# Masking the attention scores with one more matmul instead of inside the scan

## The chip, the cores and the metric

One Trainium2 chip, one core of it. The metric is the device time of one execution in microseconds (us), input and output in device memory. The kernel before takes 1345.78 us, the median of three runs.

## The reference, cut to what matters

One decoder layer on 1024 tokens of width 1024: RMS norm, a projection to six blocks of 512 columns, a short convolution on three of them and an attention with 8 heads of 64 on the other three, an output projection, then a mixture of experts. The change touches the attention alone:

```
for blk in range(S // Q_BLOCK):                       # 8 blocks of 128 queries
    z = einsum('bhqd,bhkd->bhqk', qb, kb) * scale     # keys 0 .. L-1, L = t0 + 128
    mask = s_idx < t_idx                              # strictly before the query
    log_keep = where(mask, log_sigmoid(-z), 0.0)
    shifted = concatenate([log_keep[..., 1:], 0])
    suffix = cumsum(shifted, axis=3, reverse=True)
    A = where(mask, exp(log_sigmoid(z) + suffix), 0.0)
    out = einsum('bhqk,bhkd->bhqd', A, vb)
```

So the weight of key s for query t is sigmoid(z_s) times the product of sigmoid(-z_j) over s < j < t, and zero for s >= t. The mask cuts only the last 128 keys of a block of queries, the ones at its diagonal.

## The kernel before

The program is a row of blocks with a barrier between them: projections with the attention, output projection with the router, dispatch, experts, combination. The first block holds all that the change touches.

The attention is cut into 64 units. Unit n belongs to a pair of heads p = n // 16, a block of queries t = n % 16 // 2 and a head h = n % 2 of the pair. Its length is (t + 1) * 128 keys: eight units of each length from 128 to 1024. For each unit

- TensorE computes the scores (`scores`, L442 to L444): three matmuls for each stretch of at most 512 keys (high by high, high by low, low by high part of the float32 values), with the 64 rows of one head as contraction. The last stretch is 128, 256, 384 or 512 keys wide, and its last matmul announces the scores.
- ScalarE (`open_unit`, L586 and L587, or L593 and L594 where the two stretches don't lie side by side in PSUM) writes sigmoid(z) to `soft` and sigmoid(-z) to `kept`. For 54 of the 64 units that is one pair of instructions.
- VectorE (`weigh`) runs a scan from the last key to the first over `kept` (L735), which leaves in each column the product of all to its right, and multiplies `soft` by it (L737). The tile `start_at` has 1 at the diagonal of its last 128 columns and 0 elsewhere. The scan's state is max(kept * state, start_at) and starts at 0, so it stays 0 right of the diagonal and starts from 1 there: this is the mask. All units lie at the right end of `soft`, whose last column is set to 0 once.
- TensorE transposes the weights 128 columns at a time (`turn`, L454), ScalarE copies them out of PSUM (L602), and TensorE multiplies them with v (`values`, L464).

TensorE's order is written out by hand. In turn n it issues the scores of unit n + 1, the values of unit n - 2, the transposes of unit n - 1 and then some matmuls of the input projection (`project`, L406, 128x512), of which a table deals out 10, 11, 16 or 20 to a turn and none to the last four. At one place in each pair of heads (`JOIN`) the norms of the next pair's q and k and of finished rows are made: TensorE sums them (L416, L422, L429), ScalarE changes its table of functions (L501) and takes logarithms and exponentials, and the scores of the next units wait there.

At the start of the program GpSimd makes the constants (L335 to L347); TensorE and ScalarE wait for seven steps of it.

Of the kernel before, what the change touches and what calls it, by code (L numbers as in the profile page):

```python
# [14 lines left out]
F32 = mybir.dt.float32  # L15
F32R = mybir.dt.float32r
# [27 lines left out]
def hymba_moe_layer(nc, x, norm_mix_w, w_in, conv_w, q_norm_w, k_norm_w, group_norm_conv_w,  # L44
                    group_norm_attn_w, w_out, norm_ffn_w, w_group, b_group, w_expert, b_expert,
                    w1, w3, w2, out):
    S, D = x.shape[1], x.shape[2]
# [30 lines left out]
    with ExitStack() as ctx:  # L78
        sem = lambda name: ctx.enter_context(nc.semaphore(name))
# [2 lines left out]
        psf = ps.rearrange("p a b -> p (a b)")  # L82

        base = (nc.sbuf_base + 31) // 32 * 32
        ROOM = 207 * KIB
        ctx.enter_context(nc.sbuf_tensor("arena", [P, ROOM // 4], F32))
        names = set()

# [27 lines left out]
        q_lo = [at(f"q_lo{i}", 84 + 16 * i, [P, S], F32R) for i in range(2)]  # L116
        k_hi = [at(f"k_hi{i}", 88 + 16 * i, [P, S], F32R) for i in range(2)]
# [3 lines left out]
        soft = [at(f"soft{i}", 112 + 4 * i, [P, S]) for i in range(2)]  # L121
        kept = [at(f"kept{i}", 120 + 4 * i, [P, S]) for i in range(2)]
# [59 lines left out]
        consts_in = sem("consts_in")  # L182
        g1_in = sem("g1_in")
        consts_made = sem("consts_made")
        soft_ends = sem("soft_ends")
# [40 lines left out]
        z_read = sem("z_read")  # L226
        multiplied = sem("multiplied")
        weighed = sem("weighed")
# [58 lines left out]
        with nc.Block(no_gpsimd_drain=True) as block:  # L287
# [44 lines left out]

            @block.gpsimd
            def _(pool):
                pool.memset(start_at, 0.0).then_inc(consts_made, 1)  # L335
                pool.memset(same_head, 0.0).then_inc(consts_made, 1)
                for b in range(2):
                    pool.memset(soft[b][:, S - 1:S], 0.0).then_inc(soft_ends, 1)
                pool.memset(eps, EPS).then_inc(consts_made, 1)
                pool.memset(u[:, 0:TAPS - 1], 0.0).then_inc(consts_made, 1)  # L340
                pool.wait_ge(consts_made, 4)
                pool.affine_select(out=ident, in_=ident, compare_op=ALU.not_equal, fill=1.0, base=0,
                                   pattern=[[-1, P]], channel_multiplier=1).then_inc(consts_made, 1)
                pool.wait_ge(consts_made, 5)
                pool.memset(same_head[0:HD, 0:HD], 1.0).then_inc(consts_made, 1)
                pool.wait_ge(consts_made, 6)
                pool.memset(same_head[HD:P, HD:P], 1.0).then_inc(consts_made, 1)  # L347
                pool.wait_ge(consts_made, 7)

                def chunk_hi(c):  # L350
                    pool.wait_ge(w_landed[c % 2], 16 * (c // 2 + 1))
                    pool.tensor_copy(w_hi[c % 2], w_raw[c % 2]).then_inc(w_hi_made, 1)

                def keys_hi(r):
                    pool.wait_ge(k_scaled, r + 1)
                    pool.tensor_copy(k_hi[r % 2], k_new[r % 2]).then_inc(k_hi_made, 1)

                for c in range(PRE):
                    chunk_hi(c)
                for p in range(NPAIR):  # L360
                    keys_hi(p)
                    for c in range(PRE + 4 * p, PRE + 4 * p + 4):
                        chunk_hi(c)
                for c in range(2 * CB):
                    if c % 2 == 0:
                        pool.wait_ge(w_out_in[c // 2], 16)
                    pool.tensor_copy(w_out_hi[:, c], w_out_raw[:, c]).then_inc(w_out_hi_made, 1)

            @block.tensor
            def _(pe):  # L370
# [60 lines left out]
                def scores(n):  # L431
                    p, t, h = n // PU, n % PU // 2, n % 2
                    rows = slice(h * HD, (h + 1) * HD)
                    cols = slice(t * P, (t + 1) * P)
                    if n % PU == 0:
                        pe.wait_ge(k_ready, p + 1)
                    for c0 in range(0, length(n), BANK):
                        c1 = min(c0 + BANK, length(n))
                        use = z_first[n] + c0 // BANK
                        pe.wait_ge(z_read, use - 2)  # L440
                        z = Z(use)[:, 0:c1 - c0]
                        pe.matmul(z, q_hi[p % 2][rows, cols], k_hi[p % 2][rows, c0:c1], start=True, stop=False)  # L442
                        pe.matmul(z, q_hi[p % 2][rows, cols], k_lo[p % 2][rows, c0:c1], start=False, stop=False)
                        mm = pe.matmul(z, q_lo[p % 2][rows, cols], k_hi[p % 2][rows, c0:c1], start=False, stop=True)  # L444
                    mm.then_inc(scored, 1)

                def turn(n):
                    pe.wait_ge(weighed, n + 1)
                    for hf in range(halves(n)):
                        g = th[n] + hf  # L450
                        if g >= 2:
                            pe.wait_ge(turned_read, g - 1)
                        for j in range(4 * hf, min(4 * hf + 4, length(n) // P)):
                            mm = pe.transpose(TB(g)[:, (j % 4) * P:(j % 4 + 1) * P], soft[n % 2][:, S - length(n) + j * P:S - length(n) + (j + 1) * P], ident)  # L454
                        mm.then_inc(turned, 1)

                def values(n):
# [10 lines left out]
                pe.wait_ge(consts_made, 7)  # L468
                turn_x(0)
                for m in range(NT):  # L470
                    if m + 1 < NT:
# [27 lines left out]
            def _(act):  # L499
# [74 lines left out]
                def open_unit(n):  # L574
                    p, t, h = n // PU, n % PU // 2, n % 2
                    act.wait_ge(scored, n + 1)
                    if n % PU == 0:
                        act.wait_ge(q_minus_made, p + 1)
                    if n >= 2:
                        act.wait_ge(turned, th[n - 1])  # L580
                    up, down = q_scale[p % 2][:, t, h:h + 1], q_minus[p % 2][:, t, h:h + 1]
                    s, k = soft[n % 2][:, S - length(n):], kept[n % 2][:, S - length(n):]
                    b = z_first[n] % 3
                    if b + halves(n) <= 3:
                        z = psf[:, b * BANK:b * BANK + length(n)]
                        act.activation(s[:, 0:length(n) - 1], z[:, 0:length(n) - 1], ACT.Sigmoid, scale=up)  # L586
                        act.activation(k, z, ACT.Sigmoid, scale=down).then_inc(z_read, halves(n))  # L587
                    else:
                        for hf in range(2):
                            c0, c1 = hf * BANK, min((hf + 1) * BANK, length(n))  # L590
                            z = Z(z_first[n] + hf)
                            last = min(c1, length(n) - 1)
                            act.activation(s[:, c0:last], z[:, 0:last - c0], ACT.Sigmoid, scale=up)  # L593
                            act.activation(k[:, c0:c1], z[:, 0:c1 - c0], ACT.Sigmoid, scale=down).then_inc(z_read, 1)  # L594

                def take_turned(n):
                    for hf in range(halves(n)):
# [11 lines left out]
                act.wait_ge(consts_made, 7)  # L609
                square_x(0)  # L610
                square_x(1)
                for i in range(4):
# [46 lines left out]
            def _(dve):  # L659
# [65 lines left out]
                        dve.scalar_tensor_tensor(y_mix[:, row], y_mix[:, row], row_gain(row), sq, ALU.mult, ALU.mult).then_inc(rows_scaled, 1)  # L725

                def weigh(n):

                    L = length(n)
                    s, k, one = soft[n % 2][:, S - L:], kept[n % 2][:, S - L:], start_at[:, S - L:]  # L730
                    if n == 0:
                        dve.wait_ge(soft_ends, 2)
# [845 lines left out]
```

## Time and profile before

| | before |
|---|---|
| median of 3 runs | 1345.78 us (1343.4 to 1346.09) |
| the profiled execution's own time | 1346.09 us |
| its span, first to last instruction | 1344.4 us |
| TensorE busy | 1196.3 us, 89% |
| VectorE busy | 870.1 us, 65% |
| ScalarE busy | 732.0 us, 54% |
| GpSimd busy | 146.7 us, 11% |

The time of an execution is some 1.7 us more than its span. A matmul is busy from its start to its modelled end, and neighbours overlap: what a matmul costs TensorE in a stream is the distance from its start to the start of the next, not its duration. The attention's units run from 116 to 546 us of the span; the experts take most of the time from 620 us on.

### The profile page before, as it was taken

The page shows a single profiled execution, that of the slowest core. Times are in us where ns is not written, and L with a number is a line of the kernel's source. Part 1 is how long each engine was busy: PE and PEld are TensorE (multiplying, and loading weights), DVE is VectorE, ACT ScalarE, POOL GpSimd, SP SyncE. Part 2 cuts the span into 40 slices and gives each one's busy share as a digit, 9 for nine tenths or more (in the row PEclk, how much of TensorE's full clock was granted, in tenths as well). Part 3 has the DMA queues.
Part 4 walks back from the last instruction along what each step waited for, and adds up shares of the span by engine and source line. Part 5 has one row for each costly group of instructions (what it writes and reads, how often), then busy time and mean ns, then how long its engine had stood idle before and what let it go on. Part 6 is the DMA issues. An engine that isn't in the chain of part 4 may idle for free. (4 is left out here: it accounts for less than half of the span.)

```text
span 1344.4 us, 16647 instructions
## 1 busy us (share of the span) xinstructions
PE 1196.3 (89%) x5806; PEld 968.3 (72%) x5806; DVE 870.1 (65%) x910; ACT 732.0 (54%) x918; POOL 146.7 (11%) x193
## 2 busy tenths in 40 slices
PE   5999979969989997899837999999999999999930
PEld 4887767747767775688716888888888888888820
DVE  4414444435435453723166999999999999999926
ACT  4322534543454236211206888888888888888810
POOL 1000000000000003100010111111111111111000
PEclk9999989979999999899857999999999999999975
DMA  6111100100000003611155999999999999999409
GB/s 203 37 32 32 32 16 16 32 16 17 16 16 23 28 14 125 265 49 48 39 249 196 357 389 384 381 382 380 384 384 385 382 386 378 384 384 388 174 17 374
DMA packets 57338, 261.88 MB, mean 195 GB/s; under 512 B 13008, under 2 KB 33488, under 8 KB 43984
## 3 DMA queue, kind: packets, MB, share of 16 engines
q1 hardware_dynamic: 46928, 240.31, 46.9%
q0 software_dynamic: 9216, 16.80, 3.3%
q10 hardware_dynamic: 1152, 4.19, 0.8%
q8 instruction: 28, 0.46, 0.1%
q14 instruction: 14, 0.11, 0.0%
HBM read 252.88 MB, written 25.17 MB: 207 GB/s over the span
## 5 line engine op out<-in xcount | busy, mean ns | idle before, releaser
L1250 DVE TENSOR_TENSOR e_lo<-W,e_hi 128x1024 fp32r<-128x1024 f32 x384 | 452.6, 1221 | 25.6 <-ACT e_hi L1244 22.5
L1244 ACT ACTIVATE e_hi<-W 128x1024 fp32r<-128x1024 f32 x384 | 403.3, 1060 | 96.8 <-PE ps L1215 94.0
L735 DVE TENSOR_TENSOR_SCAN kept<-kept,start_at 128x128 f32<-128x128 f32 (+7 forms) x64 | 88.7, 1385 | 210.7 <-ACT kept L587 177.6
L1213 PE MATMUL ps<-e_hi,xT_hi 128*128 128x512 f32 x512 | 204.2, 399 | 7.1 <-DVE e_lo L1250 7.1
L1215 PE MATMUL ps<-e_lo,xT_hi 128*128 128x512 f32 x512 | 201.5, 394 | 0.0
L1214 PE MATMUL ps<-e_hi,xT_lo 128*128 128x512 f32 x512 | 201.0, 393 | 0.0
L406 PE MATMUL ps<-xnT_hi,w_hi 128*128 128x512 f32 x320 | 128.4, 401 | 15.2 <-DVE u L699 7.1
L586 ACT ACTIVATE soft<-ps,q_scale 128x127 f32<-128x127 f32 (+7 forms) x54 | 38.0, 704 | 186.4 <-PE ps L454 175.6
L406 PE MATMUL ps<-xnT_hi,w_lo 128*128 128x512 f32 x320 | 127.9, 400 | 0.0
L406 PE MATMUL ps<-xnT_lo,w_hi 128*128 128x512 f32 x320 | 127.7, 399 | 0.0
L1213 PEld LDWEIGHTS ps<-e_hi,xT_hi 128*128 128x128 f32 x512 | 97.6, 191 | 27.0 <-issue 4.0
L1215 PEld LDWEIGHTS ps<-e_lo,xT_hi 128*128 128x128 f32 x512 | 97.1, 190 | 20.9
L1214 PEld LDWEIGHTS ps<-e_hi,xT_lo 128*128 128x128 f32 x512 | 97.2, 190 | 19.4
L1213 PE MATMUL ps<-e_hi,hidT_hi 128*128 128x512 f32 x256 | 103.0, 403 | 2.7 <-DVE e_lo L1250 2.7
L1215 PE MATMUL ps<-e_lo,hidT_hi 128*128 128x512 f32 x256 | 100.4, 392 | 0.0
L1214 PE MATMUL ps<-e_hi,hidT_lo 128*128 128x512 f32 x256 | 100.4, 392 | 0.0
L464 PE MATMUL ps<-probsT,v 128*64 128x128 f32 x576 | 84.5, 297 | 9.7 <-ACT probsT L602 9.7
L464 PEld LDWEIGHTS ps<-probsT,v 128*64 128x64 f32 x576 | 68.2, 148 | 26.3 <-issue 12.5
L1307 POOL DMA_INDIRECT y_rows<-y,idx_pair x32 | 32.6, 1020 | 458.4 <-ACT y L1270 458.4
L406 PEld LDWEIGHTS ps<-xnT_hi,w_hi 128*128 128x128 f32 x320 | 60.8, 190 | 28.1 <-issue 16.6
L406 PEld LDWEIGHTS ps<-xnT_lo,w_hi 128*128 128x128 f32 x320 | 61.0, 191 | 11.8 <-issue 0.2
L406 PEld LDWEIGHTS ps<-xnT_hi,w_lo 128*128 128x128 f32 x320 | 61.0, 191 | 11.7
(207 smaller groups left out, 1768.2 us busy)
## 6 DMA issues: line engine op xcount, KB each, us to landing
W<-in_w_dram SPq DMA_DIRECT2D x96, 2048.0 KB, 10.7
w_raw<-in_w_in_dram SPq DMA_DIRECT2D x20, 512.0 KB, 4.0
yy<-y_rows SPq DMA_DIRECT2D x8, 1024.0 KB, 13.6
xt<-in_x_dram SPq DMA_DIRECT2D x8, 512.0 KB, 3.8
w_out_raw<-in_w_out_dram SPq DMA_DIRECT2D x4, 1024.0 KB, 9.4
xn_rows<-xn SPq DMA_DIRECT2D x8, 512.0 KB, 2.6
out_dram<-x ACTq DMA_DIRECT2D x8, 512.0 KB, 9.0
x<-in_x_dram SPq DMA_DIRECT2D x1, 3072.0 KB, 14.9
```

Of the source, the lines that this page charges most:

```text
L406: mm = pe.matmul(ps[:, 6 + g % 2], w, r, start=(i % TICKS == 0), stop=(i % TICKS == TICKS - 1))
L464: mm = pe.matmul(ps[h * HD:(h + 1) * HD, VB, (t % 4) * P:(t % 4 + 1) * P], v[:, j, head], probsT[:, j, :], start=(j == 0), stop=(j == t))
L586: act.activation(s[:, 0:length(n) - 1], z[:, 0:length(n) - 1], ACT.Sigmoid, scale=up)
L735: dve.tensor_tensor_scan(back, back, one[:, ::-1], 0.0, ALU.mult, ALU.max).then_inc(multiplied, 1)
L1213: pe.matmul(o, xs_hi[:, k], e_hi[:, p, cols], start=(k == 0), stop=False)
L1214: pe.matmul(o, xs_lo[:, k], e_hi[:, p, cols], start=False, stop=False)
L1215: mm = pe.matmul(o, xs_hi[:, k], e_lo[:, p, cols], start=False, stop=(k == last))
L1244: act.activation(e_hi[:, p], flat[:, p * D:(p + 1) * D], ACT.Copy).then_inc(s["hi_made"], 1)
L1250: dve.tensor_tensor(e_lo[:, p], flat[:, p * D:(p + 1) * D], e_hi[:, p], ALU.subtract).then_inc(s["lo_made"], 1)
L1307: pool.indirect_dma_start(out=y_rows, out_offset=bass.IndirectOffsetOnAxis(ap=idx_pair[b].bitcast(U32), axis=0), in_=y[b], in_offset=None, ...
```

## The change

The mask moves from VectorE's scan to TensorE. Two more constants are made, `identr` (the identity) and `maskr` (-1e30 on and above the diagonal, 0 below), both 128x128 in the type fp32r that the scores' matmuls use. Behind the scores of each unit one more matmul adds `maskr` to the last 128 columns: the masked scores are so low that sigmoid(z) is 0 and sigmoid(-z) is 1 there. The scan then starts at 1, has `kept` as both operands and takes the minimum (of a product and one of its factors, which is the product). `start_at` and the semaphore `soft_ends` go; units lie at the left end of `soft` and `kept`; the arena is 2 KiB smaller. The waits for the constants go from 7 to 10.

```
-        start_at = keep("start_at", [P, S])
-        ident = start_at[:, S - P:S]
+        ident = keep("ident", [P, P])
         same_head = keep("same_head", [P, P])
+        identr = keep("identr", [P, P], F32R)
+        maskr = keep("maskr", [P, P], F32R)
...
-                pool.memset(start_at, 0.0).then_inc(consts_made, 1)
+                pool.memset(ident, 0.0).then_inc(consts_made, 1)
+                pool.memset(maskr.bitcast(F32), 0.0).then_inc(consts_made, 1)
...
+                pool.wait_ge(consts_made, 8)
+                pool.tensor_copy(identr, ident).then_inc(consts_made, 1)
+                pool.affine_select(out=maskr, in_=maskr.bitcast(F32), compare_op=ALU.is_gt, fill=MASKED, base=0,
+                                   pattern=[[-1, P]], channel_multiplier=1).then_inc(consts_made, 1)
...
-                        mm = pe.matmul(z, q_lo[p % 2][rows, cols], k_hi[p % 2][rows, c0:c1], start=False, stop=True)
+                        pe.matmul(z, q_lo[p % 2][rows, cols], k_hi[p % 2][rows, c0:c1], start=False, stop=(c1 < length(n)))
+                    mm = pe.matmul(z[:, c1 - c0 - P:c1 - c0], identr, maskr, start=False, stop=True)
                     mm.then_inc(scored, 1)
...
-                        act.activation(s[:, 0:length(n) - 1], z[:, 0:length(n) - 1], ACT.Sigmoid, scale=up)
-                        act.activation(k, z, ACT.Sigmoid, scale=down).then_inc(z_read, halves(n))
+                        act.activation(soft[n % 2][:, 0:length(n)], z, ACT.Sigmoid, scale=up)
+                        act.activation(kept[n % 2][:, 0:length(n)], z, ACT.Sigmoid, scale=down).then_inc(z_read, halves(n))
...
-                    back = k[:, ::-1]
-                    dve.tensor_tensor_scan(back, back, one[:, ::-1], 0.0, ALU.mult, ALU.max).then_inc(multiplied, 1)
+                    back = k[:, L - 1::-1]
+                    dve.tensor_tensor_scan(back, back, back, 1.0, ALU.mult, ALU.min).then_inc(multiplied, 1)
                     dve.wait_ge(multiplied, n + 1)
-                    dve.tensor_tensor(s[:, :L - 1], s[:, :L - 1], k[:, 1:], ALU.mult).then_inc(weighed, 1)
+                    dve.tensor_tensor(s[:, :L - 1], s[:, :L - 1], k[:, 1:L], ALU.mult).then_inc(weighed, 1)
```

## Rows read from the trace of the kernel before

**Rows 1.** The page's 40 slices of the span: TensorE busy and its granted clock.
```profile
PE   5999979969989997899837999999999999999930
PEclk9999989979999999899857999999999999999975
```

**Rows 2.** Busy time by stretch, four stretches of the attention; columns in the first row.
```profile
core 0: us, PE busy (x) PEld busy (x) DVE busy (x) ACT busy (x) POOL busy (x), PEclk, DMA share, GB/s
...
201.00:262.00 61.00, 60.66 (x333) 46.62 (x331) 27.64 (x29) 27.93 (x55) 2.08 (x2) 1.00 0.09 25
262.00:312.00 50.00, 38.86 (x165) 28.84 (x166) 17.82 (x15) 21.96 (x34) 3.40 (x3) 0.80 0.04 12
...
410.00:511.00 101.00, 100.67 (x542) 78.70 (x541) 51.27 (x50) 36.00 (x67) 5.50 (x4) 1.00 0.07 22
511.00:547.00 36.00, 25.97 (x132) 19.05 (x130) 15.78 (x11) 22.50 (x32) 13.36 (x9) 0.86 0.25 102
```

**Rows 3.** Who waited for whom: TensorE, 110 to 546 us; total, times, longest.
```profile
PE ps L464 <- ACT probsT L602: 9.7, 7, 3.9
PE ps L442 <- ACT kept L587: 8.2, 2, 4.1
```

**Rows 4.** The timeline of TensorE's matmuls, one unit of 640 keys: start, duration.
```profile
146.30 0.39 PE L444 MATMUL ps<-k_hi,q_lo 64*128 64x512 f32 x1
146.53 0.22 PE L442 MATMUL ps<-k_hi,q_hi 64*128 64x128 f32 x1
146.59 0.27 PE L443 MATMUL ps<-k_lo,q_hi 64*128 64x128 f32 x1
146.70 0.27 PE L444 MATMUL ps<-k_hi,q_lo 64*128 64x128 f32 x1
146.90 0.87 PE L464 MATMUL ps<-probsT,v 128*64 128x128 f32 x6
```

**Rows 5.** The timeline of the weight loads in the same unit.
```profile
146.30 0.18 PEld L442 LDWEIGHTS ps<-k_hi,q_hi 64*128 64x128 f32 x1
146.53 0.18 PEld L443 LDWEIGHTS ps<-k_lo,q_hi 64*128 64x128 f32 x1
146.64 0.19 PEld L444 LDWEIGHTS ps<-k_hi,q_lo 64*128 64x128 f32 x1
```

**Rows 6.** The timeline of TensorE's matmuls where a unit's last stretch is 512 wide.
```profile
240.69 0.39 PE L444 MATMUL ps<-k_hi,q_lo 64*128 64x512 f32 x1
241.01 0.65 PE L464 MATMUL ps<-probsT,v 128*64 128x128 f32 x4
```

**Rows 7.** The timeline at the second pair's join; the wait before stands in brackets.
```profile
284.74 0.90 ACT L586 ACTIVATE soft<-ps,q_scale 128x767 f32<-128x767 f32 x1
...
286.48 0.68 PE L442 MATMUL ps<-k_hi,q_hi 64*128 64x384 f32 x1 [4.08 <-ACT kept L587]
286.96 0.52 PE L443 MATMUL ps<-k_lo,q_hi 64*128 64x384 f32 x1
287.28 0.52 PE L444 MATMUL ps<-k_hi,q_lo 64*128 64x384 f32 x1
```

**Rows 8.** Groups of instructions by line and shape, 90 to 560 us: VectorE's `weigh`.
```profile
L735 DVE TENSOR_TENSOR_SCAN kept<-kept,start_at 128x1024 f32<-128x1024 f32 x8 | 18.4, 2299 | 26.2 <-ACT kept L587 21.1 <-ACT kept L594 5.1
...
L737 DVE TENSOR_TENSOR soft<-soft,kept 128x1023 f32<-128x1023 f32 x8 | 10.4, 1306 | 0.3
...
L735 DVE TENSOR_TENSOR_SCAN kept<-kept,start_at 128x128 f32<-128x128 f32 x8 | 5.0, 625 | 16.2 <-ACT kept L587 16.2
```

**Rows 9.** The timeline of the program's start.
```profile
0.84 0.95 POOL L335 MEMSET start_at<- 128x1024 f32 x1 [0.29 <-POOLq L1573]
...
2.31 0.28 POOL L342 TENSOR_SCALAR_AFFINE_SELECT start_at<-start_at 128x128 f32<-128x128 f32 x1 [0.24 <-POOL u L340]
...
2.86 0.15 POOL L347 MEMSET same_head<- 64x64 f32 x1
...
4.08 1.28 ACT L506 ACT_TABLE_LOAD   x1 [4.08 <-DMA xt<-in_x_dram]
```

More of the change, by code:

```diff
@@ L184, in hymba_moe_layer @@
         consts_made = sem("consts_made")
-        soft_ends = sem("soft_ends")
         x_landed = [sem(f"x_landed{i}") for i in range(2)]
@@ L334, in _ @@
             def _(pool):
-                pool.memset(start_at, 0.0).then_inc(consts_made, 1)
+                pool.memset(ident, 0.0).then_inc(consts_made, 1)
+                pool.memset(maskr.bitcast(F32), 0.0).then_inc(consts_made, 1)
                 pool.memset(same_head, 0.0).then_inc(consts_made, 1)
-                for b in range(2):
-                    pool.memset(soft[b][:, S - 1:S], 0.0).then_inc(soft_ends, 1)
                 pool.memset(eps, EPS).then_inc(consts_made, 1)
                 pool.memset(u[:, 0:TAPS - 1], 0.0).then_inc(consts_made, 1)
-                pool.wait_ge(consts_made, 4)
+                pool.wait_ge(consts_made, 5)
                 pool.affine_select(out=ident, in_=ident, compare_op=ALU.not_equal, fill=1.0, base=0,
                                    pattern=[[-1, P]], channel_multiplier=1).then_inc(consts_made, 1)
-                pool.wait_ge(consts_made, 5)
+                pool.wait_ge(consts_made, 6)
                 pool.memset(same_head[0:HD, 0:HD], 1.0).then_inc(consts_made, 1)
-                pool.wait_ge(consts_made, 6)
+                pool.wait_ge(consts_made, 7)
                 pool.memset(same_head[HD:P, HD:P], 1.0).then_inc(consts_made, 1)
-                pool.wait_ge(consts_made, 7)
+                pool.wait_ge(consts_made, 8)
+                pool.tensor_copy(identr, ident).then_inc(consts_made, 1)
+                pool.affine_select(out=maskr, in_=maskr.bitcast(F32), compare_op=ALU.is_gt, fill=MASKED, base=0,
+                                   pattern=[[-1, P]], channel_multiplier=1).then_inc(consts_made, 1)
                 def chunk_hi(c):
@@ L453, in turn @@
                         for j in range(4 * hf, min(4 * hf + 4, length(n) // P)):
-                            mm = pe.transpose(TB(g)[:, (j % 4) * P:(j % 4 + 1) * P], soft[n % 2][:, S - length(n) + j * P:S - length(n) + (j + 1) * P], ident)
+                            mm = pe.transpose(TB(g)[:, (j % 4) * P:(j % 4 + 1) * P], soft[n % 2][:, j * P:(j + 1) * P], ident)
                         mm.then_inc(turned, 1)
@@ L466, in values @@
                     mm.then_inc(valued, 1)
-                pe.wait_ge(consts_made, 7)
+                pe.wait_ge(consts_made, 10)
                 turn_x(0)
@@ L581, in open_unit @@
                     up, down = q_scale[p % 2][:, t, h:h + 1], q_minus[p % 2][:, t, h:h + 1]
-                    s, k = soft[n % 2][:, S - length(n):], kept[n % 2][:, S - length(n):]
                     b = z_first[n] % 3
@@ L585, in open_unit @@
                         z = psf[:, b * BANK:b * BANK + length(n)]
-                        act.activation(s[:, 0:length(n) - 1], z[:, 0:length(n) - 1], ACT.Sigmoid, scale=up)
-                        act.activation(k, z, ACT.Sigmoid, scale=down).then_inc(z_read, halves(n))
+                        act.activation(soft[n % 2][:, 0:length(n)], z, ACT.Sigmoid, scale=up)
+                        act.activation(kept[n % 2][:, 0:length(n)], z, ACT.Sigmoid, scale=down).then_inc(z_read, halves(n))
                     else:
                         for hf in range(2):
[L590 to L594, printed above, removed]
+                            cols = slice(hf * BANK, min((hf + 1) * BANK, length(n)))
+                            z = Z(z_first[n] + hf)[:, 0:cols.stop - cols.start]
+                            act.activation(soft[n % 2][:, cols], z, ACT.Sigmoid, scale=up)
+                            act.activation(kept[n % 2][:, cols], z, ACT.Sigmoid, scale=down).then_inc(z_read, 1)
                 def take_turned(n):
@@ L727, in weigh @@
                 def weigh(n):
[L729 to L732, printed above, removed]
+                    s, k, L = soft[n % 2], kept[n % 2], length(n)
                     dve.wait_ge(z_read, z_first[n] + halves(n))
-                    back = k[:, ::-1]
-                    dve.tensor_tensor_scan(back, back, one[:, ::-1], 0.0, ALU.mult, ALU.max).then_inc(multiplied, 1)
+                    back = k[:, L - 1::-1]
+                    dve.tensor_tensor_scan(back, back, back, 1.0, ALU.mult, ALU.min).then_inc(multiplied, 1)
                     dve.wait_ge(multiplied, n + 1)
-                    dve.tensor_tensor(s[:, :L - 1], s[:, :L - 1], k[:, 1:], ALU.mult).then_inc(weighed, 1)
+                    dve.tensor_tensor(s[:, :L - 1], s[:, :L - 1], k[:, 1:L], ALU.mult).then_inc(weighed, 1)
                 dve.wait_ge(g1_in, 16)
```

4 lines of the change are left out of this document (2 added, 2 removed).

## The prediction, made before the changed kernel was run

> **What bounds the kernel now.** I read the page's slices first, for where TensorE is full and at which clock. It is busy nine tenths and more of most slices, with dips in the attention's part [rows 1]. The stretches tell the two kinds of attention apart: from 201 to 262 us TensorE is busy 60.66 of 61.00 us, from 410 to 511 us 100.67 of 101.00, both at granted clock 1.00 (2.4 GHz), while VectorE and ScalarE are busy at most half of the time. From 262 to 312 us and from 511 to 547 us, a join and the end, it is busy 38.86 of 50.00 and 25.97 of 36.00 us, at 0.80 and 0.86, a mix of 2.4 and 1.2 GHz [rows 2]. So in the plain run of units TensorE sets the pace and a nanosecond added to its stream is a nanosecond of time, and VectorE's scan is off the path. At the joins and at the end the pace is that of a chain through ScalarE and VectorE. The view of waits says the same: TensorE's long waits are few, two of 4.1 us each for `kept` and seven for `probsT` with 9.7 us in all [rows 3].
>
> What a small matmul costs must come from starts. The timeline of one unit of 640 keys shows all the cases. The 512-wide L444 is followed by the next start after 0.23 us (146.30 to 146.53). The first 128-wide one, whose weights were loaded while L444 ran (load at 146.30), is followed after 0.06 us (146.53 to 146.59). The next is followed after 0.11 us (146.59 to 146.70), as its own weights could only be loaded behind that one (load at 146.53, the next at 146.64). The last is followed after 0.20 us by the values, which stand behind a wait [rows 4, 5]. That wait costs 0.09 us over the stream: a 512-wide L444 in front of it is followed after 0.32 us (240.69 to 241.01) instead of 0.23 [rows 4, 6].
>
> **The change, part by part.**
>
> *The extra matmul, 64 times.* It has 128 columns and the full 128x128 weights. Nothing stands between L444 and it, so its weights can load while L444 runs, as those of the 128-wide L442 did. Behind it stands the wait that stood behind L444.
>
> - Last stretch 256, 384 or 512 wide (48 units): L444 is long enough to hide the load of 0.11 us, so the extra matmul adds its own streaming, 0.06 us. 48 x 0.06 = 2.9 us.
> - Last stretch 128 wide (16 units, lengths 128 and 640): L444 is too short to hide it, and the pace is 0.11 us. 16 x 0.11 = 1.8 us.
>
> Together 4.7 us. Off this go units whose extra matmul falls into a wait. At the join L444 of one unit ends long before ScalarE opens it at 284.74 us, and TensorE then waits 4.08 us [rows 7]: one such unit at each of the three joins with a next pair (the fourth has none behind it), and two at the end, where the turns have no projection to do and TensorE idles 10 us [rows 2]. 5 x 0.06 = 0.3 us off. To it come the units that run at half clock behind such a wait, where 384 columns take 0.32 us (286.96 to 287.28) [rows 7]; that is 0.11 us for 128 columns instead of 0.06. Some six of them, 6 x 0.05 = 0.3 us. The two cancel, and the sum stays at 4.7 us.
>
> The bounds: if every one of the 64 costs the load's pace, 64 x 0.11 = 7.0 us. If only the streaming counts and all of some 15 units around the joins and at the end are covered, 49 x 0.06 = 2.9 us. Neither holds a penalty for going from 64 rows of contraction to 128 and back. The trace has such a step only across a wait (L444 to L464), at the same 0.09 us that L444 of any width pays there, so I take none. The upper end keeps it: the load exposed behind L444 adds another 64 x 0.11, for 0.06 + 0.11 = 0.17 us a unit, 10.9 us.
>
> Of this load the Trainium skill ("TensorE: Matmul & The Clock Gate", section "The mechanism") says that it overlaps a running matmul only when the two use different row groups. The trace speaks against it: L442's 64-row load starts at 146.30, together with the 64-row L444, and its matmul follows at L444's full pace [rows 4, 5]. By the skill's rule the load would be exposed each time, which is the 10.9 us of the rival below; by the row it is hidden.
>
> *The longer chain.* The scores are announced 0.06 to 0.11 us later. ScalarE doesn't wait for them in the plain run: it opens a unit when the transposes two units back are done, which TensorE issues behind these scores and the values. Those cover it, and ScalarE is busy 27.93 of 61.00 us there [rows 2]. Where the cover is gone, at the joins, the extra matmul is in the sum already.
>
> *ScalarE.* One column more in 64 of its instructions (128x1024 for 128x1023): nothing that a row can show, and behind TensorE.
>
> *The scan.* Same length, same number of streams read, same start and end. It takes 2299 ns for 1024 columns and L737 1306 ns for 1023 with as many operands [rows 8]. Going from 128 to 1024 columns costs 1674 ns, 1.87 ns a column. I take no change. Bounds: if reading `kept` twice brought it to L737's time, 1.0 us less for the longest; if a clash of the two reads cost as much, 1.0 us more. In the plain run either is hidden behind TensorE; it counts only at the joins and the end, for two or three scans each, 10 scans in all and so at most 10 us either way.
>
> *The constants.* GpSimd's first memset of 0.95 us shrinks to an eighth of its columns, and one memset, one copy and one select of 128 columns come, the select at 0.28 us by its like. GpSimd's last step ended at 3.01 us, and ScalarE's first work waits for x until 4.08 us [rows 9]. Three steps of at most 0.3 us, even without the saving, end by 3.91 us: nothing. Without that cover it would be 0.1 us, 0.9 less the 0.8 saved. VectorE's wait for `soft_ends` had long been met.
>
> *After the attention.* The next block begins behind a barrier, and the experts' weights are asked for there, so the delay is passed on whole.
>
> **The sum.** 1346.09 us of the profiled execution plus 4.7 is 1350.8. That execution is the slowest of three, 0.3 us over their median of 1345.78, so I forecast 1350.5 us. About 0.2%, 2.7 us, is what a measurement of this kernel can tell from no change.
>
> **The rivals.**
>
> - *The load is not hidden.* L444 uses 64 rows, `identr` all 128; if the weights can't go in while a matmul on part of the rows runs, each unit costs 0.17 us: 10.9 us, 1356.7. For it: no row shows a step from 64 to 128 rows without a wait. Against it: the loads of rows 5 run under matmuls on the same rows. It decides from 0.11 us a unit on.
> - *It lands in slack.* TensorE idles 11.1 us in the join shown and 10.0 us at the end [rows 2], with two more joins at most some 43 us, and a delay in front of a wait can be absorbed. If a third of the extra matmuls fell there, and the last units' turns were paced by ScalarE, 43 x 0.06 = 2.6 us would be left: within 0.2%, 1348.4. For it: the waits of rows 3. Against it: they sit at four places, and rows 2 give TensorE 99.4% and more between them.
> - *The scan gets shorter* (the other side). If its pace is set by reading two tiles, reading one tile twice could bring it to 1306 ns. The joins and the end are chains through it: 10 scans x 1.0 us = 10 us off, plus 4.7, is 1340.5. It decides once a long scan loses over 0.7 us. Against it: L737 also reads two tiles, one column a step, in 1306 ns, so the reading of two tiles is not what makes 2299.
>
>   The Trainium skill ("DVE: opcode table, instruction layouts, handler registers and perf-mode slots", section "Datapath and trigger behaviour") says that the scan routes its state back a stage and runs at half throughput; the trace agrees in direction, with 1.87 ns a column against at most 1.28 (1306 / 1023) for L737. By that rule nothing about the operands helps, and the scan stays at 2299.
>
> **Chances.** The sum as worked out 0.55; the load exposed, or a like penalty for the step in rows, 0.17; slack 0.22; a shorter scan or another gain 0.06. The forecast is the first. The first case has its own range from 1348.7 (2.9 us) to 1352.8 (7.0 us). For 8 in 10 the range must reach into slack below and most of the way to the exposed load above: 1347.0 to 1357.0. Slower by over 0.2%: the first two cases, 0.72. Within 0.2%: 0.22. Faster: 0.06.
>
> **What the profile after would show.** 64 more matmuls of 128x128 with a start 0.23 us behind a 512-wide L444, and the values 0.15 us behind them (0.20 behind a 128-wide L444). If the load is exposed, its start lies 0.34 us behind. The scans at 2299 and 625 ns, by length. The first values matmul of the stretch from 410 to 511 us comes later by as many small steps as units lie before it, and the block's end by 4 to 5 us; after that every stage keeps its length. The prediction is wrong if the scan changes by over 0.1 us, if the waits of rows 3 shrink by what the matmuls add, or if the clock at a join falls or rises at another place: 10 us of full-clock work that runs at half clock instead costs 10 us more.

## The result, and the profile after

The changed kernel takes 1354.05 us, the median of 5 runs (1353.19 to 1359.11), where the kernel before takes 1345.36 us beside it. The ratio is 1.0081, with a 95% interval of 1.0057 to 1.0104. That is 8.7 us slower. I had forecast 1350.5 us in a range from 1347.0 to 1357.0, so the direction and the range held, and the cost is almost twice the 4.7 us of the sum.

The page of the changed kernel, its slices as in [rows 1]:

```profile
span 1359.5 us, 16775 instructions
PE   6999989979998998799945999999999999999930
PEclk9999969988998998899956999999999999999975
```

The profiled execution took 1361.15 us, the longest of those seen, 15.1 us over that of before. So the span can't be compared with the median above; why executions of this kernel differ so much is taken up with the experiments. The stretches of [rows 2], in the changed kernel:

```profile
core 0: us, PE busy (x) PEld busy (x) DVE busy (x) ACT busy (x) POOL busy (x), PEclk, DMA share, GB/s
...
160.00:201.00 41.00, 35.31 (x147) 27.21 (x146) 13.47 (x12) 15.12 (x25) 3.27 (x3) 0.76 0.05 14
201.00:262.00 61.00, 60.88 (x324) 46.54 (x322) 26.44 (x27) 27.04 (x55) 2.86 (x2) 0.99 0.06 18
...
410.00:511.00 101.00, 96.32 (x497) 74.70 (x498) 50.05 (x48) 36.48 (x67) 6.29 (x4) 0.97 0.07 21
```

TensorE is as full as before from 201 to 262 us, with fewer matmuls in the stretch (324 for 333). The units are the same, so each takes longer. The stretch from 410 to 511 us now holds part of a join, which has moved later, and can't be compared with its row of before. The last step of the attention, ScalarE's copy of the last output, shows the sum of it, in the timeline of before and then of the changed kernel:

```profile
545.96 0.60 ACT L607 ACTIVATE y_mix<-ps 128x512 f32<-128x512 f32 x1 [2.05 <-PE ps L464]
```

```profile
563.22 0.60 ACT L607 ACTIVATE y_mix<-ps 128x512 f32<-128x512 f32 x1 [2.05 <-PE ps L466]
```

The attention ends 17.3 us later. The spans differ by 15.1 us, so 2.2 us come back in the stages behind. There the trace has TensorE at half clock for 114.6 us before and for 109.9 us here. By the two levels these 4.7 us are worth at most 2.3 us, near the difference; more on this stands with the second profile below.

The timeline of TensorE's matmuls in the unit of 640 keys, as in [rows 4], tells what the extra matmul (L446) costs:

```profile
146.69 0.39 PE L445 MATMUL ps<-k_hi,q_lo 64*128 64x512 f32 x1
146.92 0.22 PE L443 MATMUL ps<-k_hi,q_hi 64*128 64x128 f32 x1
146.98 0.27 PE L444 MATMUL ps<-k_lo,q_hi 64*128 64x128 f32 x1
147.09 0.27 PE L445 MATMUL ps<-k_hi,q_lo 64*128 64x128 f32 x1
147.29 0.33 PE L446 MATMUL ps<-maskr,identr 128*128 128x128 f32 x1
147.55 0.87 PE L466 MATMUL ps<-probsT,v 128*64 128x128 f32 x6
```

And the weight loads there, as in [rows 5]:

```profile
147.03 0.19 PEld L445 LDWEIGHTS ps<-k_hi,q_lo 64*128 64x128 f32 x1
147.29 0.19 PEld L446 LDWEIGHTS ps<-maskr,identr 128*128 128x128 f32 x1
```

L446 starts 0.20 us behind L445, as the values did before it, and the values start 0.26 us behind L446. No wait stands in front of L446, and still its load begins only at 147.29, with the matmul itself, and not under L445. In a unit whose last stretch is 384 wide the two steps are 0.26 and 0.26 us:

```profile
243.15 0.33 PE L445 MATMUL ps<-k_hi,q_lo 64*128 64x384 f32 x1
243.41 0.33 PE L446 MATMUL ps<-maskr,identr 128*128 128x128 f32 x1
243.67 0.65 PE L466 MATMUL ps<-probsT,v 128*64 128x128 f32 x4
```

So a unit pays 0.26 us whatever its width, and 64 of them 16.6 us. TensorE's waits, as in [rows 3], have shrunk (the view goes from 110 to 560 us):

```profile
PE ps L466 <- ACT probsT L602: 7.7, 4, 3.6
...
PE ps L443 <- ACT kept L588: 6.9, 2, 3.4
```

The attention ends at 564 us here, and up to there `probsT` has 8.3 us in 5 waits. So the two shrank by 1.4 and 1.3 us, and all rows of this view together from 36.7 us to 31.4.

The scan of 1024 columns kept its length, 2364 ns on the mean where [rows 8] have 2299. That of 128 columns has a mean of 736 ns for 625, over the 0.1 us that I had named as a sign of being wrong. But most single ones take 0.42 us in both kernels, and the mean is moved by a few long ones (two of 1.2 us before; four of 0.8 to 1.3 us here), whose number differs from profile to profile. The second experiment shows that the scan costs no time.

### The profile page after: what moved, and what is told of

The parts are those of the page before. It is cut to its first block and busy times, and to the rows that moved or that the text cites. A ratio compares the mean times of both kernels' runs of the same rounds, so it can differ in the third digit from the quotient of the medians.

```text
span 1359.5 us, 16775 instructions
## 1 busy us (share of the span) xinstructions
PE 1218.1 (90%) x5870; PEld 984.5 (72%) x5870; DVE 871.8 (64%) x910; ACT 732.6 (54%) x918; POOL 146.9 (11%) x194
## 5 line engine op out<-in xcount | busy, mean ns | idle before, releaser
L731 DVE TENSOR_TENSOR_SCAN kept<-kept 128x128 f32<-128x128 f32 (+7 forms) x64 | 91.0, 1422 | 228.6 <-ACT kept L588 191.7
L587 ACT ACTIVATE soft<-ps,q_scale 128x128 f32<-128x128 f32 (+7 forms) x54 | 38.1, 705 | 200.4 <-PE ps L456 189.2
L407 PE MATMUL ps<-xnT_hi,w_hi 128*128 128x512 f32 x320 | 128.9, 403 | 14.4 <-DVE u L699 6.9
L353 POOL CAST w_hi<-w_raw 128x1024 fp32r<-128x1024 f32 x20 | 24.8, 1238 | 421.7 <-DMA w_raw<-in_w_in_dram 421.7
```

The costliest lines, as they stand in the source:

```text
L407: mm = pe.matmul(ps[:, 6 + g % 2], w, r, start=(i % TICKS == 0), stop=(i % TICKS == TICKS - 1))
L587: act.activation(soft[n % 2][:, 0:length(n)], z, ACT.Sigmoid, scale=up)
L731: dve.tensor_tensor_scan(back, back, back, 1.0, ALU.mult, ALU.min).then_inc(multiplied, 1)
```

## The experiments

**Which part costs.** The first kernel adds only the extra matmul and its constants to the kernel before. The second takes only the extra matmul out of the changed kernel.

```
# e1, on the kernel before
-                        mm = pe.matmul(z, q_lo[p % 2][rows, cols], k_hi[p % 2][rows, c0:c1], start=False, stop=True)
+                        pe.matmul(z, q_lo[p % 2][rows, cols], k_hi[p % 2][rows, c0:c1], start=False, stop=(c1 < length(n)))
+                    mm = pe.matmul(z[:, c1 - c0 - P:c1 - c0], identr, maskr, start=False, stop=True)

# e2, on the changed kernel
-                        pe.matmul(z, q_lo[p % 2][rows, cols], k_hi[p % 2][rows, c0:c1], start=False, stop=(c1 < length(n)))
-                    mm = pe.matmul(z[:, c1 - c0 - P:c1 - c0], identr, maskr, start=False, stop=True)
+                        mm = pe.matmul(z, q_lo[p % 2][rows, cols], k_hi[p % 2][rows, c0:c1], start=False, stop=True)
```

> The kernel before with the extra matmul and its two constants alone; scan, alignment and start_at as before. Theory A (the extra matmul is all of the loss; it starts 0.20 us behind a 128-wide last matmul and 0.32 us behind a 512-wide one, as if a wait stood between, and is followed after 0.26 us): the same gaps, attention's end 16 to 18 us later than before in the profiled execution, and the time that of the changed kernel within 2 us, 1352 to 1360 us. Theory B (a part of the loss lies in the scan's new operands or the left alignment): the same gaps, but at least 3 us less time than the changed kernel.

> The changed kernel without the extra matmul: the mask is left out of the computation, so keys at and behind the diagonal count. Theory A: 1344 to 1347 us, as before, and scans as in the changed kernel (2.3 us for 1024 columns). Theory B: 3 us or more over before.

With the matmul alone: 1356.97 us, ratio 1.0098 (1.0081 to 1.0115). Without it: 1343.67 us beside 1343.83 of before, ratio 0.9999 (0.9989 to 1.0009). The gaps of the first are those expected (0.20, 0.32 and 0.26 us). Two numbers of theory A were missed: its median lies 2.9 us over that of the changed kernel, where I had allowed 2, and its attention ends 15.3 us later than before, not 16 to 18. B wanted a shorter time than the changed kernel's, so A holds. The scan's new operands and the left alignment cost nothing that can be measured, nor do the constants; the extra matmul is the whole loss.

**Why 0.26 us.** In the third kernel the extra matmul contracts over the head's 64 rows, as the scores do:

```
-                    mm = pe.matmul(z[:, c1 - c0 - P:c1 - c0], identr, maskr, start=False, stop=True)
+                    mm = pe.matmul(z[:, c1 - c0 - P:c1 - c0], identr[rows], maskr[rows], start=False, stop=True)
```

> The extra matmul contracts over the 64 rows of the head instead of 128: half of the queries' masks are left out, and the instruction count stays. Theory C (the step from 64 to 128 rows is what keeps the weights from loading early): the extra matmul starts 0.23 us behind a 512-wide one and is followed after 0.15 us, 0.06 to 0.11 us a unit, some 5 us in all, 1349 to 1352 us. Theory D (any short matmul behind the scores costs this, by its width or its constant operands): 0.26 us a unit as in the changed kernel, 1353 us or more.

1348.01 us, ratio 1.0035 (1.0021 to 1.0049), 4.2 us more than before. Its timeline, same unit:

```profile
145.64 0.27 PE L444 MATMUL ps<-k_lo,q_hi 64*128 64x128 f32 x1
145.75 0.27 PE L445 MATMUL ps<-k_hi,q_lo 64*128 64x128 f32 x1
145.87 0.27 PE L446 MATMUL ps<-maskr,identr 64*128 64x128 f32 x1
146.07 0.87 PE L466 MATMUL ps<-probsT,v 128*64 128x128 f32 x6
```

0.12 us to L446 and 0.20 from it: where one step of 0.20 us stood there are now two, and the unit pays 0.11 to 0.12 us. In units with a wider last stretch it pays 0.06 us (behind a 512-wide L445 the steps are 0.23 and 0.15 us, where one of 0.32 stood). These are the prices of my sum, and the total of 4.2 us is near its 4.7, if 1 us under the range of theory C. With one shape for the scores and the extra matmul the sum is right; what was wrong is that a change of shape is free. Theory C holds over D, which would have the same loss here.

The fourth kernel moves the full matmul between the values (128x64) and the transposes (128x128):

```
+                def mask(n):
+                    wide = length(n) - (halves(n) - 1) * BANK
+                    z = Z(z_first[n] + halves(n) - 1)
+                    pe.matmul(z[:, wide - P:wide], identr, maskr, start=False, stop=True).then_inc(scored, 1)
...
                     if n >= 2:
                         values(n - 2)
+                    if r != JOIN[p] + 1 and n + 1 < UNITS:
+                        mask(n + 1)
                     if n:
                         turn(n - 1)
```

> The extra matmul of each unit moved behind the values (128 rows, 64 columns) and ahead of the transposes (128 rows); it computes the same. Theory C: no step in rows is added, its weights load under the values, and it costs 0.06 to 0.11 us a unit: 1349 to 1352 us. Theory D: 0.26 us a unit, 1353 us or more. By either, ScalarE opens its units no later, as it waits for the transposes behind.

1352.18 us, ratio 1.0061 (1.0041 to 1.0080), between the two theories' ranges. The timeline (L450 is the extra matmul):

```profile
244.04 0.65 PE L469 MATMUL ps<-probsT,v 128*64 128x128 f32 x4
244.62 0.33 PE L450 MATMUL ps<-maskr,identr 128*128 128x128 f32 x1
244.79 0.41 PE L459 MATMUL ps<-ident,soft 128*128 128x128 f32 x2
```

L450 starts 0.58 us behind the values and stands 0.17 us ahead of the transposes. But the transposes behind it are shortened: before, they stood first behind the values, and the second of them followed the first after 0.16 us; here it follows after 0.13. Over the whole turn, from its first scores matmul to its third projection matmul, it is 2.46 us where before has 2.32:

```profile
240.12 0.49 PE L442 MATMUL ps<-k_hi,q_hi 64*128 64x512 f32 x1
...
241.59 0.55 PE L454 MATMUL ps<-start_at,soft 128*128 128x128 f32 x3
...
242.44 0.39 PE L406 MATMUL ps<-xnT_hi,w_hi 128*128 128x512 f32 x1
```

The unit pays 0.13 us, and 64 of them 8.5 us, near the measured loss of 8.4 us.

Theory C as I had put it, the step in rows alone, is too narrow. The values and L450 both have 128 rows, but the values load 64 columns of weights and L450 loads 128, and L450's load isn't hidden: it starts only with the matmul, at 244.62. The kernel before has this change too, in front of its transposes. So L450 adds no change, it only moves to where one is.

The 0.09 us that I had put down to waits doesn't belong to them either. Between L450 and the transposes stands a wait for VectorE, and the step is 0.17 us, the load's 0.11 and the streaming's 0.06, without the 0.09. In the changed kernel no wait stands between L445 and L446, and there the 0.09 us is paid (0.32 us behind a 512-wide one for 0.23). What stands at both places where it was paid, here and in [rows 4, 6], is a change of shape. The kernel before had shown a wait without the price, even in the rows that I had read: its code has a wait for ScalarE (`z_read`) in front of each stretch of scores, so also in front of the L442 at 146.53 us, and that starts after the plain 0.23 us [rows 4]. It is the same at 163.52 us, behind another wait for ScalarE and with one shape on both sides:

```profile
163.29 0.40 PE L406 MATMUL ps<-xnT_lo,w_hi 128*128 128x512 f32 x1
163.52 0.84 PE L416 MATMUL ps<-same_head,q_sq 128*128 128x2 f32 x7
```

So, theory E: each change of shape costs 0.09 us and a weight load in the open, whether there is a wait or not. The Trainium skill says the first half of it: "Changing tiling mode (not just tile) drains the TensorE" ("TensorEngine Tiling (Array Packing)", section "Key Properties", under "Tiling Modes"). The trace agrees, and its price here is 0.09 us for the drain, up to 0.11 us more for the load of 128 columns and 0.05 us for one of 64. This page spoke against the change, and I hadn't weighed it.

The next two kernels put the extra matmul where both neighbours are 128x128: behind the transposes, and behind the first projection matmul of the turn.

```
# e5
                     if n:
                         turn(n - 1)
+                    if r != JOIN[p] + 1 and n + 1 < UNITS:
+                        mask(n + 1)
                     project(ticks_by(n - 1), ticks_by(n))

# e6
+                    first = min(ticks_by(n - 1) + 1, ticks_by(n))
+                    project(ticks_by(n - 1), first)
+                    if r != JOIN[p] + 1 and n + 1 < UNITS:
+                        mask(n + 1)
+                    project(first, ticks_by(n))
```

> The extra matmul moved behind the transposes and ahead of the projection; both are 128x128, and it computes the same. Theory E (each change of the tile's shape on TensorE costs a start delayed by 0.09 us and a weight load of 0.11 us that isn't hidden, wait or no wait; the extra matmul between 64x128 and 128x64 adds one such change): here it adds none and costs only the pace of a weight load, 0.11 us a unit; 64 x 0.11 = 7.0 us at most, 1348 to 1352 us. Theory W (the 0.09 us is the price of a wait and only a step in rows hides no load): as before the move behind the values, 0.16 us a unit, 1352 us or more.

> The extra matmul moved behind the first projection matmul of the turn, 512 wide, under which its weights load. Theory E: 0.06 us a unit, some 3.5 us in all, 1346 to 1349 us, less than behind the transposes. Theory W: 0.11 us or more a unit, 1350 us or more.

Behind the transposes: 1348.75 us, ratio 1.0031 (1.0017 to 1.0044), in E's range and under W's. The same unit as above, from its scores to the third projection matmul, takes 2.43 us for 2.32:

```profile
239.53 0.49 PE L443 MATMUL ps<-k_hi,q_hi 64*128 64x512 f32 x1
...
241.00 0.55 PE L459 MATMUL ps<-ident,soft 128*128 128x128 f32 x3
241.31 0.31 PE L450 MATMUL ps<-maskr,identr 128*128 128x128 f32 x1
241.45 0.44 PE L407 MATMUL ps<-xnT_lo,w_hi 128*128 128x512 f32 x1
241.73 0.39 PE L407 MATMUL ps<-xnT_hi,w_lo 128*128 128x512 f32 x1
241.96 0.40 PE L407 MATMUL ps<-xnT_hi,w_hi 128*128 128x512 f32 x1
```

That is E's 0.11 us a unit. In the projection: 1354.01 us, ratio 1.0070 (1.0052 to 1.0088). This is over E's range; by the letter it is W's expectation that came in, though W is out by the step from L445 to L446. Its timeline:

```profile
241.60 0.48 PE L407 MATMUL ps<-xnT_lo,w_hi 128*128 128x512 f32 x1
241.91 0.22 PE L450 MATMUL ps<-maskr,identr 128*128 128x128 f32 x1
241.97 0.44 PE L407 MATMUL ps<-xnT_hi,w_lo 128*128 128x512 f32 x1
242.25 0.39 PE L407 MATMUL ps<-xnT_hi,w_hi 128*128 128x512 f32 x1
```

The extra matmul is followed after 0.06 us, as expected. But the next one, 512 wide, is followed after 0.28 us and not 0.23: its weights had only 0.06 us of cover. In a stream of one shape the price of a short matmul is the pace of a load, 0.11 us; a wide one in front only moves it to the one behind. (In e3 it was 0.06 us, but there a change of shape stood behind it, whose load is in the open anyway.) That makes it equal to e5, and not 5 us worse. Most of the 5 us goes with the clock, which comes below.

The eighth kernel issues the extra matmul twice in a row:

> Two extra matmuls in a row behind the scores (the mask is added twice, which computes the same). Theory E: the second adds no change of shape, only the pace of a weight load, 0.11 us a unit, 5 to 7 us over the changed kernel. Theory D (each such matmul costs 0.26 us by itself): 14 to 17 us over it.

1360.05 us, ratio 1.0111 (1.0093 to 1.0130): 5.5 us over the same kernel with one, timed beside it, at a higher mean granted clock (0.945 against 0.943). Its timeline:

```profile
246.52 0.39 PE L445 MATMUL ps<-k_hi,q_lo 64*128 64x512 f32 x1
246.84 0.33 PE L446 MATMUL ps<-maskr,identr 128*128 128x128 f32 x1
247.01 0.28 PE L447 MATMUL ps<-maskr,identr 128*128 128x128 f32 x1
247.22 0.65 PE L467 MATMUL ps<-probsT,v 128*64 128x128 f32 x4
```

From the first extra matmul to the values it is now 0.38 us (0.17 and 0.21) where it was 0.26, 0.12 more: the first carries its own load and its streaming, the second the pace of a load, and the drain is paid once. D, 0.26 us for each, is out.

One table puts the prices together by the turn, so without the clock's share. It compares the turns that run outside the joins, 52 of them, each with the same turn of the kernel before, from the first scores matmul to the third projection matmul; the second column is the turn shown above, of a unit with 512 keys.

| | that turn | over before, median of 52 | times 64 | median time over before |
|---|---|---|---|---|
| before | 2.32 us | | | |
| changed kernel | 2.58 us | 0.26 us | 16.6 us | 8.7 and 9.7 us |
| e3, 64 rows | 2.38 us | 0.06 us | 4.6 us, with 0.11 for 16 of them | 4.2 us |
| e4, behind the values | 2.46 us | 0.13 us | 8.5 us | 8.4 us |
| e5, behind the transposes | 2.43 us | 0.11 us | 7.2 us | 3.9 us |
| e6, in the projection | 2.43 us | 0.11 us | 7.0 us | 9.2 us |
| e8, twice | 2.68 us | 0.36 us | 23.3 us | 15.2 us |

Without the extra matmul (e2) the median over before is 0. The last two columns differ by what waits take up and by the clock.

**Why executions differ.** The changed kernel was run again.

> The changed kernel once more, for another profile. Theory G (its executions differ, 1353 to 1361 us, by how long TensorE's clock is granted at half): an execution near 1354 us has a mean granted clock of 0.944 to 0.945 and in its profile some 10 us less at half clock, in the attention or right behind it; one near 1360 us has 0.938. Theory H (they differ by something else, as transfers): times and clock don't go together.

1354.58 us, ratio 1.0071 (1.0053 to 1.0089). Here are all ten executions of the changed kernel, profiled ones included, with the mean granted clock of each:

```
us      1353.19 1353.79 1353.81 1354.05 1354.53 1354.64 1356.99 1358.26 1359.11 1361.15
clock   0.944   0.944   0.945   0.944   0.944   0.943   0.942   0.941   0.940   0.938
```

They go together, with a correlation of -0.98, and 0.001 of clock is worth 1.2 us. That is near what the two levels give: 0.001 of 1355 us is 2.7 us more at 1.2 GHz, and each such microsecond of full work costs half a microsecond more, 1.4 us. The kernel before stays between 0.939 and 0.942 in all 13 executions timed beside these, 1344.8 us on the mean. Its own times there, 1342.1 to 1347.5 us, don't go with the clock; in the two other groups of its executions, with clocks from 0.937 to 0.945, they do in part (correlations -0.60 and -0.73). At its 0.940 to 0.941 the changed kernel takes 1358.3 to 1359.1 us, 13.5 to 14.4 us more than before. The median shows 8.7 because more than half of the executions were granted the full clock for longer.

The second profile, of the execution of 1356.99 us, shows where. The same stretch as above, the first join:

```profile
160.00:201.00 41.00, 34.62 (x158) 26.32 (x157) 15.13 (x13) 17.23 (x28) 4.06 (x3) 0.88 0.05 14
```

Clock 0.88 for 0.76 is 10 us less at half clock ((0.88 - 0.76) x 2 x 41), and 11 more matmuls fit into the stretch. In the first profile TensorE runs at half clock twice here, for 6.8 us from 178 us on and for 13.7 us from 188 us on; in the second once, for 10.2 us from 187 us on. In both it had idled 0.46 us just before 178 us, and only in one did the clock fall there. Theory G holds. What decides it in an execution isn't settled: the program is the same. It also explains most of e6: its four executions had 0.939 to 0.940, those of e5 0.943 on the mean, which is 4 us.

The second profile also compares best with that of before, whose clock in this stretch is 0.88 too:

```profile
160.00:201.00 41.00, 33.98 (x163) 25.99 (x162) 16.63 (x15) 16.43 (x28) 3.74 (x3) 0.88 0.05 14
```

In both traces TensorE is at half clock for 47.8 us of the attention. The attention ends 13.5 us later (559.48 us for 545.96), the 16.6 us of the extra matmuls less what the waits take up. The stages behind it come in two lengths in the 13 profiles of this record, 798.0 to 798.4 us with 114.2 to 114.6 us at half clock and 795.7 to 796.2 us with 109.9 to 110.6 us. The profile of before has the long one, that of the changed kernel the short one both times. It isn't the extra matmul that decides it: e6, which has it, and e2, which hasn't, both have the long one.

**A version with fewer changes of shape.** A turn of the kernel before goes 128x128 (projection), 64x128 (scores), 128x64 (values), 128x128 (transposes): three changes, 64 times. The last three kernels leave mask and scan as before and do the two heads of one block of queries in the same turn where the buffers allow it: the values of units up to 512 keys (their transposed weights share one tile, half each), the scores of units of 256 to 512 keys, and both.

```
# e9: values of two heads
+        in_pair = lambda n: n % PU < 8
+        probs_at = lambda n: 4 * (n % 2) if in_pair(n) else 0
...
-                        values(n - 2)
+                        if not in_pair(n - 2):
+                            values(n - 2)
+                        elif n % 2:
+                            values(n - 3)
+                            values(n - 2)
...
-                            act.wait_ge(valued, n)
+                            act.wait_ge(valued, n - 1 if 1 <= n % PU < 8 else n)

# e10: scores of two heads
...
+                    pe.wait_ge(z_read, z_first[n + 1] - 2)
+                    for term, (q, k) in enumerate(((q_hi, k_hi), (q_hi, k_lo), (q_lo, k_hi))):
+                        for h in range(2):
+                            rows = slice(h * HD, (h + 1) * HD)
+                            mm = pe.matmul(Z(z_first[n + h])[:, 0:length(n)], q[p % 2][rows, cols], k[p % 2][rows, 0:length(n)],
+                                           start=(term == 0), stop=(term == 2))
...
```

> The kernel before, mask in the scan, with the values of two heads done in one turn for units of up to 512 keys; the same instructions, 16 changes of tile shape fewer (128x64 between 64x128 and 128x128). Theory E (a change of shape costs a start delayed by 0.09 us and a load that isn't hidden, 0.05 us for 64 columns): 0.14 us a pair, 2.2 us less attention in the profile, in equal steps of 0.14 us; the time 1342 to 1344 us where before gives 1345. Theory W (the price belongs to the waits): as many waits are left out, so this gives the same; against it speaks that transposes to projection has a wait and no price. If nothing is gained, the price is hidden by something else.

> The kernel before with the scores of both heads in one turn for the 24 units of 256 to 512 keys that share a block of queries, their matmuls taking turns between the upper and the lower 64 rows. Theory E: 12 changes of shape fewer at 0.20 us, 2.4 us less. Theory R (matmuls on different halves of the rows run side by side, as the two starts 0.05 us apart at the join of the kernel before): another 0.35 to 0.69 us a pair, 6 us, so 8 us less in all, about 1337 us. Without R, 1342 to 1343 us.

> Both together. By E and R the two gains add, 10 to 11 us less attention in the profile and a time near 1335 us; by E without R 4 to 5 us less. If ScalarE or VectorE becomes the bound for the short units, less than the sum of the two.

| | median | ratio to before | interval |
|---|---|---|---|
| values in pairs | 1338.97 us | 0.9949 | 0.9932 to 0.9967 |
| scores in pairs | 1334.25 us | 0.9922 | 0.9898 to 0.9946 |
| both | 1326.25 us | 0.9865 | 0.9839 to 0.9890 |

All three are faster than both kernels, the last by 18.8 us than before. The gains add up, or a little more. Each is larger than expected. For the scores I had expected both heads to run side by side, and they do: six matmuls take the 0.89 us that three took (237.39 to 238.28), two starting together.

```profile
237.39 0.50 PE L454 MATMUL ps<-k_hi,q_hi 64*128 64x512 f32 x2
237.72 0.40 PE L454 MATMUL ps<-k_lo,q_hi 64*128 64x512 f32 x2
237.96 0.39 PE L454 MATMUL ps<-k_hi,q_lo 64*128 64x512 f32 x2
238.28 0.65 PE L476 MATMUL ps<-probsT,v 128*64 128x128 f32 x4
```

For the values I had counted only the changes of shape, 2.2 us. The timeline of the kernel with values in pairs shows the rest:

```profile
235.22 0.67 PE L466 MATMUL ps<-probsT,v 128*64 128x128 f32 x8
235.82 0.55 PE L456 MATMUL ps<-start_at,soft 128*128 128x128 f32 x3
```

Eight matmuls of two heads take 0.60 us, where four of one head took 0.58 in the kernel before (from 241.01 us [rows 6] to the transposes at 241.59) and in e4: heads that write different halves of the output partitions run side by side too, even though the program issues all of one head first. The Trainium skill says that different tiles load and multiply in parallel (same page, same section); the trace agrees, 8 in 0.60 us. For longer units less of it overlaps: the 12 matmuls of two heads with 384 keys take 1.08 us where six took 0.80, and the 16 of two heads with 512 keys 1.51 us where eight took 1.02. A pair saves 0.36, 0.57, 0.52 and 0.52 us from 128 to 512 keys, 7.9 us for all 16. The median gained 6.1 us, at a mean clock 0.001 under that of before. With both in pairs there is one more gain: 12 turns then have neither scores nor values, so no change of shape at all, and their transposes start 0.23 us behind the last projection matmul. So these three kernels don't price a change of shape alone; the changed kernel, e3 and e8 do.

## Why the prediction was right, and where it was off

- *TensorE sets the pace in the plain run of units.* Right. The whole loss came from its stream, and e2 shows that nothing else of the change costs time.
- *The price of the extra matmul.* This is the step that failed: "Nothing stands between L444 and it, so its weights can load while L444 runs", and with it "That wait costs 0.09 us over the stream". There is a change of shape between them. It costs 0.09 us, and the load is in the open. The term that I put at 0.06 to 0.11 us measured 0.26 us (0.09 + 0.11 + 0.06), and 64 x 0.26 is 16.6 us where the sum had 4.7. I read the 0.09 us rightly from [rows 4, 6] but gave it to the wait, because in those rows the wait and the change of shape stand in the same place. A row with only one of the two was in rows 4 themselves: the L442 at 146.53 us stands behind a wait and pays nothing for it.
- *"I take none" for the step in rows.* The argument was that L444 to the values pays 0.09 us at any width. It does, and that was the penalty itself, of which the change adds one more.
- *The rival "the load is not hidden".* Nearest to what happened, at 0.17 us a unit and 10.9 us; it lacks the drain. Its reason, the row groups, is refuted by the loads that overlap in one shape ([rows 5]) and by e4, where the rows are the same and the load is still in the open.
- *What waits take up.* I took off 0.3 us. The two kinds of wait in [rows 3] alone shrank by 2.7 us, all of TensorE's waits in the attention by 5.3 us.
- *The clock.* The prediction's last sentence names it as what would make it wrong, with 10 us at half clock. In the profiled execution the first join has some 10 us more of it than before; most other executions had a mean clock over that of before, which hid some 5 us of the loss in the median. This isn't in the sum, and without it the time would have been outside the range, near 1359. A price that was 3.5 times too low was offset in part by waits and clock that the sum didn't have: that the range held is luck.
- *Scan, ScalarE, constants, passing the delay on.* Right: e2 for the first three. For the last, the attention ends 17.3 us later and the span 15.1; the 2.2 us between them go with TensorE's clock in the stages behind, not with the change.

## What to carry to other kernels

Count a kernel's changes of tile shape on TensorE, rows by columns of the weights, before counting its matmuls: one costs 0.14 to 0.20 us here, where a 512-wide matmul takes 0.23, and a small matmul of another shape put between two groups adds one. Put small extra work next to a group of its own shape, and put groups of one shape together, above all those on different halves of rows or columns, which then run side by side. When a gap has two possible causes in one row, look for a row that has only one of them before pricing it; and compare executions at the same mean granted clock where a kernel has stalls in front of full TensorE work.

## What the runs showed of the hardware that was not expected

- A wait that is met costs TensorE nothing in a stream (0.23 us from a 512-wide matmul to the next across one); a change of the weights' shape costs 0.09 us, and the next weights load in the open, 0.11 us for 128 columns.
- Two matmuls on different halves of the rows start together (e10), and runs of 128x64 matmuls on different halves of the columns overlap though one run is issued whole before the other (8 in 0.60 us where 4 take 0.58; 16 in 1.51 us where 8 take 1.02).
- Executions of one kernel differ by 8 us together with the granted clock: 1353.19 us at 0.944, 1361.15 us at 0.938, correlation -0.98 over ten.
